# A decoder layer on one core: first stage in half chunks, gate sigmoids at the copies, HGRN products in 64x64 blocks, and moved transfers

## What is computed

```
ada = silu(c) @ w_ada + b_ada                      # sh1 sc1 gt1 sh2 sc2 gt2
h = x*(1+sc1) + sh1
qa ka va hq hf hi hg ga gb = split(h @ w_in)       # 7 x 512, 2 x 1024 columns
ya = attention(qa, ka, va)                         # 8 heads x 64, causal, ALiBi
yb = hgrn2(hq, hf, hi, hg)                         # 4 heads, chunks of 64 tokens, 128x128 state
mixed = sigmoid(ga)*(ya @ w_branch_a) + sigmoid(gb)*(yb @ w_branch_b)
x = layer_norm(ALPHA*x + gt1*(mixed @ w_out))
h2 = x*(1+sc2) + sh2
x = layer_norm(ALPHA*x + gt2*peer(h2))             # top 16 of 128^2 experts, 8 heads
```

## Time and profile before

| | |
|---|---|
| runs | 976.68, 977.14, 977.97 us; median 977.14 |
| profiled execution | 978.03 us; span in the profile 976.3 us |
| granted TensorE clock, mean | 0.994 |
| PE busy | 956.7 us, 98% |
| DVE busy | 802.2 us, 82% |
| ACT busy | 545.0 us, 56% |
| POOL busy | 385.4 us, 39% |
| DMA | 239.57 MB, mean 245 GB/s |
| chain that ended last | PE 88%, DVE 5%, DMA 3%, ACT 2% |

### The profile page before, as it was taken

How to read it: one execution, slowest core, us unless ns; L and a number is a source line. 1 busy time by engine, 2 the same in 40 slices (tenths; PEclk the granted TensorE clock), 3 DMA queues, 4 the chain that set the end, 5 groups by cost and what they waited for, 6 DMA issues and landing times.

```text
span 976.3 us, 17754 instructions
## 1 busy us (share of the span) xinstructions
PE 956.7 (98%) x6783; PEld 886.8 (91%) x6783; DVE 802.2 (82%) x1495; ACT 545.0 (56%) x851; POOL 385.4 (39%) x234
## 2 busy tenths in 40 slices
PE   8999999999999999999999999999999999999995
PEld 7999999999999999999999999888888888888884
DVE  6979888884987989887699998788776878887866
ACT  5477656455445464546577776554445444445542
POOL 1010101002888787676877867222330322300002
PEclk9999999999999999999999999999999999999998
DMA  9988968876666787886766666899889899986761
GB/s 358 412 300 270 352 200 326 311 222 219 195 201 179 196 200 176 217 198 185 179 159 167 157 169 152 290 323 316 284 288 369 300 327 333 324 293 215 216 193 44
DMA packets 86661, 239.57 MB, mean 245 GB/s; under 512 B 26929, under 2 KB 27953, under 8 KB 84913
## 3 DMA queue, kind: packets, MB, share of 16 engines
q1 hardware_dynamic: 59536, 207.94, 63.6%
q0 software_dynamic: 26752, 30.49, 13.5%
q10 hardware_dynamic: 288, 0.01, 0.0%
HBM read 227.84 MB, written 10.55 MB: 244 GB/s over the span
## 4 chain that ended last, share of the span: by engine, by line
PE 88%; DVE 5%; DMA 3%; ACT 2%; issue 1%; SPq 1%; POOL 1%; POOLq 0%; ACTq 0%; DVEq 0%
PE px L1303 35%; PE pw L964 15%; PE pw L965 15%; PE pw L966 15%; DMA raw<-in_ws 2%; DMA raw<-in_w 2%; DVE w_lo L1365 1%; PE px L1278 1%; PE px L1270 1%; PE px L965 1%; PE px L964 1%; PE px L966 1%; ACT oh_g L637 0%; PE px L1227 0%; ACT w_hi L637 0%
## 5 line engine op out<-in xcount | busy, mean ns | idle before, releaser
L637 ACT ACTIVATE w_hi<-raw 128x1024 fp32r<-128x1024 f32 x308 | 324.8, 1059 | 277.9 <-PE px L1303 144.8
L1365 DVE TENSOR_TENSOR w_lo<-raw,w_hi 128x1024 fp32r<-128x1024 f32 x285 | 348.1, 1229 | 87.5 <-ACT w_hi L637 84.9
L964 PE MATMUL pw<-a_hi,w_hi 128*128 128x240 f32 (+1 forms) x1248 | 347.2, 278 | 0.3 <-DVE a_lo L1617 0.3
L966 PE MATMUL pw<-a_hi,w_lo 128*128 128x240 f32 (+1 forms) x1248 | 344.5, 276 | 0.0
L965 PE MATMUL pw<-a_lo,w_hi 128*128 128x240 f32 (+1 forms) x1248 | 344.5, 276 | 0.0
L589 POOL DMA_INDIRECT gates_spill<-gate,place x128 | 237.2, 1853 | 72.6 <-issue 46.7
L964 PEld LDWEIGHTS pw<-a_hi,w_hi 128*128 128x128 f32 x1248 | 236.0, 189 | 1.8 <-issue 0.7
L965 PEld LDWEIGHTS pw<-a_lo,w_hi 128*128 128x128 f32 x1248 | 236.1, 189 | 0.0
L966 PEld LDWEIGHTS pw<-a_hi,w_lo 128*128 128x128 f32 x1248 | 236.0, 189 | 0.0
L1303 PE MATMUL px<-w_hi,ws_hi 128*128 128x512 f32 x512 | 159.0, 389 | 0.0
L1303 PE MATMUL px<-w_hi,ws_lo 128*128 128x512 f32 x512 | 158.9, 389 | 0.0
(11 more groups left out here) (370 smaller groups left out, 1277.8 us busy)
## 6 DMA issues: line engine op xcount, KB each, us to landing
raw<-in_u SPq DMA_DIRECT2D x128, 512.0 KB
raw<-in_v SPq DMA_DIRECT2D x128, 512.0 KB
raw<-in_ws SPq DMA_DIRECT2D x52, 512.0 KB
ada<-in_ada SPq DMA_DIRECT2D x20, 512.0 KB, 7.5
ada<-in_w_ada SPq DMA_DIRECT2D x16, 512.0 KB, 8.6
gates_spill<-zero POOLq DMA_DIRECT2D x16, 512.0 KB, 8.1
g_row<-gates_spill SPq DMA_DIRECT2D x32, 256.0 KB
raw<-in_w SPq DMA_DIRECT2D x7, 1024.0 KB, 11.8
```

Of the source, the lines that this page charges most:

```text
L637: return nc.scalar.activation(out, in_, ACT.Copy, **kw)
L964: nc.tensor.matmul(out, lh, rh, start=start and x == 0, stop=False)
L966: last = nc.tensor.matmul(out, ll, rh, start=False, stop=stop and x == len(pairs) - 1)
L1365: v.tensor_tensor(w_lo[:, m % RING], raw[:, m % RING], w_hi[:, m % RING].bitcast(F32), ALU.subtract).then_inc(lo_ready, 1)
```

## The change

- First stage: every chunk is copied and subtracted in two halves of 1024 columns. ACT's order per chunk is first half, a_hi and xT, second half; DVE's is modulation, first half, a_lo, second half. PE waits for the first half before the chunk and for the second before `first_rows`.
- Gates: gb is put through the sigmoid where it is copied out of PSUM; ga is still copied, and one sigmoid over all of it stands in ACT's iteration 20. The two sigmoids of iteration 23 go. DVE waits for each copy of gb.
- HGRN: the product at block 12 is made as 64x64 blocks on the diagonal (16 matmuls with 64 stationary and 64 moving columns for 8 of 128x128), and the state products at block 14 alternate between the two chunks.
- Transfers: x_nat and `ln_cols` load at block 20, after `s_done` 4 in place of `pv_done` 4; the bias of gt1 at block 21. AdaLN tiles: three in block 20, one in 21, 22 and 23 (before 1, 1, 2, 2). Of the 16 clears 0 to 6 stay; 7 to 15 are issued by POOL after each second subtraction of U, with no wait.
- `acc_lo` is made by DVE at block 21 instead of POOL. DVE's wait for the clears moves behind seven of its searches.

```diff
+X_AT = 20
...
-ADA_PER_BLOCK = {9: 2, 10: 1, 11: 1, 12: 1, 13: 1, 14: 2, 15: 2, 16: 2, 17: 2, 18: 2, 20: 1, 21: 1, 22: 2, 23: 2, 27: 1, 28: 1}
+ADA_PER_BLOCK = {9: 2, 10: 1, 11: 1, 12: 1, 13: 1, 14: 2, 15: 2, 16: 2, 17: 2, 18: 2, 20: 3, 21: 1, 22: 1, 23: 1, 27: 1, 28: 1}
...
-                    sp.wait_ge(lo1_ready, c - CHUNK_SLOTS + 2)
+                    sp.wait_ge(lo1_ready, 2 * (c - CHUNK_SLOTS) + 2)
...
-                if b == BRANCH + 2:
-                    sp.wait_ge(pv_done, HEADS // 2)
+                if b == X_AT:
+                    sp.wait_ge(s_done, HEADS // 2)
                     sp.dma_start(x_nat[:, :, :], x_d.rearrange("(a p) n -> p a n", p=P)).then_inc(x_landed, 16)
                     sp.dma_start(ln_cols[:, :], ln1_cols_d).then_inc(x_landed, 16)
+                if b == X_AT + 1:
...
-                    pool.wait_ge(lo_ready, 4 + 46 * n // ZERO_DMAS)
+                    if n < 7:
+                        pool.wait_ge(lo_ready, 4 + 46 * n // ZERO_DMAS)
...
-            clear(5, 10)
-            pool.wait_ge(o_done, TT)
-            pool.wait_ge(gt1_ready, 1)
-            nc.gpsimd.tensor_tensor(acc_lo[:, :], acc[:, :], acc_hi[:, :].bitcast(F32), ALU.subtract).then_inc(gt1_ready, 1)
-            clear(10, 12)
-
-            clear(12, 14)
+            clear(5, 7)
...
-            clear(14, ZERO_DMAS)
 
             pool.wait_ge(lo_ready, lo_count(UP - 1))
             for m in range(UP, UP + POOL_PIECES):
                 split_lo(m)
+                n = 7 + (m - UP) // 2
+                if (m - UP) % 2 and n < ZERO_DMAS:
+                    clear(n, n + 1)
...
-            def split_hi1(c):
-
-                act.wait_ge(raw1_landed[c % CHUNK_SLOTS], 16 * (c // CHUNK_SLOTS + 1))
+            def split_hi1(c, h):
+
+                q = slice(h * FW // 2, (h + 1) * FW // 2)
+                if c == 0 and h:
+                    act.wait_ge(raw1_head_landed, 16)
+                else:
+                    act.wait_ge(raw1_landed[c % CHUNK_SLOTS], 16 * (c // CHUNK_SLOTS + 1))
                 if c >= 2:
                     act.wait_ge(chunk_used, c - 1)
-                copy(hi1[c % 2][:, :], raw1[c % CHUNK_SLOTS][:, :]).then_inc(hi1_ready, 1)
+                copy(hi1[c % 2][:, q], raw1[c % CHUNK_SLOTS][:, q]).then_inc(hi1_ready, 1)
 
             for half in range(2):
                 act.wait_ge(sc_row_done, half + 1)
                 copy(sc_row[:, half * 512:(half + 1) * 512], (pw[0], px[0])[half][:, :]).then_inc(sc_row_ready, 1)
-            act.wait_ge(raw1_landed[0], 16)
-            copy(hi1[0][:, 0:FW // 2], raw1[0][:, 0:FW // 2]).then_inc(hi1_ready, 1)
             for c in range(KC):
+                split_hi1(c, 0)
                 act.wait_ge(x_chunk_landed[c], 16)
                 act.wait_ge(mod1_ready, c + 1)
                 for out in (a_hi, xT):
                     last = nc.scalar.activation(out[:, c], xT[:, c], ACT.Identity, scale=mod1[:, 2 * c + 1:2 * c + 2],
                                                 bias=mod1[:, 2 * c:2 * c + 1])
                 last.then_inc(h_hi_ready, 1)
-                if c == 0:
-                    act.wait_ge(raw1_head_landed, 16)
-                    copy(hi1[0][:, FW // 2:FW], raw1[0][:, FW // 2:FW]).then_inc(hi1_ready, 1)
-                if c + 1 < KC:
-                    split_hi1(c + 1)
+                split_hi1(c, 1)
...
-                for lo, dst in ((GA, sig_a), (GB, sig_b)):
-                    if lo <= e < lo + 4:
-                        r = e - lo
-                        copy(dst[:, 2 * r:2 * r + 2], pw[s][:, :].rearrange("p (c t) -> p c t", c=2)).then_inc(act_took, 1)
+                if GA <= e < GA + 4:
+                    r = e - GA
+                    copy(sig_a[:, 2 * r:2 * r + 2], pw[s][:, :].rearrange("p (c t) -> p c t", c=2)).then_inc(act_took, 1)
+                if GB <= e < GB + 4:
+                    r = e - GB
+                    nc.scalar.activation(sig_b[:, 2 * r:2 * r + 2], pw[s][:, :].rearrange("p (c t) -> p c t", c=2),
+                                         ACT.Sigmoid).then_inc(act_took, 1)
...
-                if b == 23:
-
-                    for dst in (sig_a, sig_b):
-                        act.wait_ge(act_took, evac_count(GB + 3))
-                        last = nc.scalar.activation(dst[:, :, :], dst[:, :, :], ACT.Sigmoid)
-                    last.then_inc(gates_ready, 1)
+                if b == 20:
+                    act.wait_ge(act_took, evac_count(GA + 3))
+                    nc.scalar.activation(sig_a[:, :, :], sig_a[:, :, :], ACT.Sigmoid).then_inc(gates_ready, 1)
...
-                pe.wait_ge(lo1_ready, c + 2 if c else 1)
+                pe.wait_ge(lo1_ready, 2 * c + 1)
                 pe.wait_ge(h_lo_ready, c + 1)
                 for b in range(HI):
                     first_block(b, c)
-                if c == 0:
-                    pe.wait_ge(lo1_ready, 2)
+                pe.wait_ge(lo1_ready, 2 * c + 2)
...
-                            q = slice(h * T + t * P, h * T + (t + 1) * P)
-                            last = nc.tensor.matmul(dst[:, h * P:(h + 1) * P], k_e[:, q], q_e[:, q], start=True, stop=True)
+                            for c in range(2):
+                                q = slice(h * T + t * P + c * CH, h * T + t * P + (c + 1) * CH)
+                                last = nc.tensor.matmul(dst[c * CH:(c + 1) * CH, h * P + c * CH:h * P + (c + 1) * CH],
+                                                        k_e[:, q], q_e[:, q], start=True, stop=True)
...
-                    for n in ((0, 1) if b == 14 else (2,)):
-                        dst = pv[n % 2]
-                        pe.wait_ge(kl_ready, 2)
-                        if n == 2:
-                            pe.wait_ge(state_ready, 1)
-                        t, q = n // 2, slice((n % 2) * CH, (n % 2 + 1) * CH)
-                        for h in range(HG):
-                            last = nc.tensor.matmul(dst[:, h * P:(h + 1) * P], kl_nat[q, t, h],
+                    chunks = (0, 1) if b == 14 else (2,)
+                    pe.wait_ge(kl_ready, 2)
+                    if b == 15:
+                        pe.wait_ge(state_ready, 1)
+                    for h in range(HG):
+                        for n in chunks:
+                            t, q = n // 2, slice((n % 2) * CH, (n % 2 + 1) * CH)
+                            last = nc.tensor.matmul(pv[n % 2][:, h * P:(h + 1) * P], kl_nat[q, t, h],
                                                     vh[q, t, h * P:(h + 1) * P], start=True, stop=True)
-                        last.then_inc(ds_done, 1)
+                            if h == HG - 1:
+                                last.then_inc(ds_done, 1)
...
-            modulation(0)
-            split_lo1_half(0)
             for c in range(KC):
+                modulation(c)
+                split_lo1(c, 0)
                 h_lo(c)
-                if c == 0:
-                    split_lo1_half(1)
-                if c + 1 < KC:
-                    modulation(c + 1)
-                    split_lo1(c + 1)
+                split_lo1(c, 1)
...
+                    dve.wait_ge(act_took, evac_count(GB + e - BRANCH))
...
+                if b == 21:
+                    dve.wait_ge(gt1_ready, 1)
+                    v.tensor_tensor(acc_lo[:, :], acc[:, :], acc_hi[:, :].bitcast(F32), ALU.subtract).then_inc(gt1_ready, 1)
...
-            dve.wait_ge(zero_landed, 16 * ZERO_DMAS)
...
+            dve.wait_ge(zero_landed, 16 * ZERO_DMAS)
```

More of the change, by code:

```diff
@@ L1380, in sum_ada, with split_lo1 @@
                 ins.then_inc(ada_done, 1)
-            def split_lo1(c):
-                dve.wait_ge(hi1_ready, c + 2)
+            def split_lo1(c, h):
+                q = slice(h * FW // 2, (h + 1) * FW // 2)
+                dve.wait_ge(hi1_ready, 2 * c + h + 1)
                 if c >= 2:
                     dve.wait_ge(chunk_used, c - 1)
-                v.tensor_tensor(lo1[c % 2][:, :], raw1[c % CHUNK_SLOTS][:, :], hi1[c % 2][:, :].bitcast(F32), ALU.subtract) \
+                v.tensor_tensor(lo1[c % 2][:, q], raw1[c % CHUNK_SLOTS][:, q], hi1[c % 2][:, q].bitcast(F32), ALU.subtract) \
                     .then_inc(lo1_ready, 1)
-            def split_lo1_half(h):
-                q = slice(h * FW // 2, (h + 1) * FW // 2)
-                dve.wait_ge(hi1_ready, h + 1)
-                v.tensor_tensor(lo1[0][:, q], raw1[0][:, q], hi1[0][:, q].bitcast(F32), ALU.subtract).then_inc(lo1_ready, 1)
             def modulation(c):
```

## The result

| | before | changed |
|---|---|---|
| median of the runs made together (6 each) | 977.05 us | 984.77 us |
| lowest and highest | 976.59, 979.25 | 983.64, 986.13 |
| profiled execution (span) | 978.03 (976.3) | 984.65 (982.9) |
| mean granted TensorE clock in it | 0.994 | 0.992 |

A forecast was written before the change was run, and what follows sets the result against it. TensorE, busy 98% of the span, was taken as the bound; gains of 1.25 + 0.95 + 3.3 less 0.1 make 5.4 us off 978.03, 972.6, so a median of 971.7; range 969.8 to 975.2.

The forecast's parts named there:

- Clears in U: Nine clear issues of 0.74 us in POOL's subtraction loop: 1.2 us behind, about 4 in hand, cost 0.
- a PE wait in U: Listed sign that the forecast is wrong: PE waiting in U, where no wait for w_lo was expected.
- The slower rival: In U, each clear issue costs POOL 2.24 us, not 0.74; PE waits 10.7 us, time 982.4; chance 0.04.
- First stage: Half copies and subtractions start chunks 1 and 2 earlier; first streamed block at 59.4 against 60.67, gain 1.25 us.
- The loop: First stage, DVE and ACT: 5.81 us a round against PE's 5.71, so chunks 3 to 7 start 0.1 apart.
- the new wait: End of first stage: ACT's weight copies start at 53.7, not 52.34; PE's first block waits for the bank until 59.4.
- HGRN: Blocks 12 and 14: 64x64 products take 1.35 us, gain 0.4; alternating state products gain 0.55; together 0.95.
- The middle: Blocks 19 to 24: m_lo wait of 1.8 us and low clock of 1.5 go, gain 3.3; y_lo loses 0.1.
- the sum: Whole kernel: 1.25 + 0.95 + 3.3 - 0.1 = 5.4 us gained, median 971.7.
- The DMA relief: From 150 to 176 us the DMA loses 4 MB of 9.5; its share falls from 0.98 to near 0.6.
- the m_lo step: Around block 24: DVE starts earlier, m_lo is ready at 189.0, 1.7 us early, so PE's 1.8 us wait goes.
- A2: Follow-up theory for U: POOL instructions overlapping 0.3 to 0.4 us shut DVE out; at 0.04 to 0.1 it gets in.

The follow-up runs named there:

- experiment 1: Changed kernel with the nine late clears issued by POOL in their old places ahead of U, all else as changed: 972.39 us, ratio 0.995.
- experiment 3: Changed kernel with the nine clears of U issued from SP's queue at the same points, POOL only subtracting: 972.32 us, ratio 0.9948.
- experiment 7: Changed kernel with one added wait: POOL's 15th subtraction of U waits for DVE's gates subtraction and place computation; clears stay in U: 972.34 us, ratio 0.995.
- experiment 8: Changed kernel, clears in U, with the gates' row maximum copied to PSUM and place_f kept there: 972.54 us, ratio 0.9946.
- experiment 9: Changed kernel with the nine clears issued by POOL in its idle stretch ahead of U: 972.14 us, ratio 0.9946 of the kernel before.
- experiment 12: Kernel before with only the sigmoids, moved transfers, three adaLN tiles and acc_lo on DVE, clears in old places: 974.85 us, ratio 0.9971.
- experiment 2: Kernel before with only the nine clears moved into U and DVE's wait for the clears moved: 987.71 us, ratio 1.0092.
- experiment 4: Changed kernel with clears before U and 704-column POOL memsets in their places in U: six runs 972.1 to 972.8, four 980.0 to 980.7, ratio 0.9979.
- experiment 5: Changed kernel with clears before U and nine 960-column POOL memsets in their places in U: median 985.53 us, ratio 1.0052.
- experiment 10: Kernel before with only the first stage in halves: 975.89 us, ratio 0.9985.
- experiment 11: Kernel before with only the 64x64 HGRN blocks and the alternating state products: 976.25 us, ratio 0.9996.
- experiment 6: Changed kernel with five of the nine clears issued before U and only the last four in it: 983.01 us, ratio 1.0053.

## Why the prediction was wrong

**The step that failed** is "Clears in U": "POOL falls 0.13 back a pair, 1.2 us in all, and has about 4 us in hand ... Cost 0, covered by that lead". Its numbers held: an issue's record is 0.7 to 1.1 us but takes 0.7 from start to start, a pair of POOL's takes 5.46 for the 5.51 of the forecast, and PE never waits for a piece of POOL. What failed is the cost put at 0: it asked who waits for POOL's results and not who needs POOL to stand still. The 0.6 us pauses of the earlier trace rows were taken for slack; in the kernel before they were where the gates subtraction and `place_f` got through (275.04 to 275.43, POOL paused from 274.82 to 275.40). Shut out of them, DVE came 21.4 us late out of `place`, its weight piece 11.3 late, PE stood 10.1 and lost 2.3 more by the clock. The cost was 12.4 us. The prediction's own list of what would show it wrong had "a PE wait in U", and that is what came, on the other engine's pieces.

**The slower rival** ("The clears starve POOL", 0.04, 982.4) had the clears and nearly the size, but the wrong way round: it had DVE hold up POOL's issues, which in U took 0.90 us in the median and 1.09 at most, not 2.24. That its 10.7 us of waiting are near the measured 10.1 is chance. Of the rule that it cited from the Trainium skill (SBUF — State Buffer, the "DVE blocks DMA" trap), no run here shows the effect; here GpSimd's stream held up VectorE.

**First stage.** PE's chunks 1 and 2 at 18.05 and 24.16 (18.24 and 24.47 forecast), first streamed block 59.24 (59.4). Chunk 0 began 0.36 earlier in this run (12.07, not 12.43); counted from it the block came at 47.17, for 46.97 forecast and 48.24 before: 1.07 gained for 1.25. The loop is as forecast: `a_hi` starts every 5.8 us from chunk 3 to 7. So is the new wait: ACT copies from 53.30 in place of 52.34, and PE starts 0.14 us after ACT has emptied the bank (59.10); the profile names the DVE subtraction that ended at 59.20, but that one is not of this block. Alone the part measures 1.24, with an interval of 0.5 to 2.3; that it is so near to 1.25 is luck.

**HGRN.** The products took 1.08, not 1.35: 0.034 a record, against 0.112 for the 128x128 form. The state products took the 1.09 read from the scores. By the rows 1.3 is gained, by the medians of the runs 0.88, which its ratio does not tell from no change; forecast 0.95. The products' cost was taken 0.3 too high. The factors are 1.7 and 1.5, under the 2 that the Trainium skill (TensorEngine Tiling (Array Packing), Theoretical Speedup) gives as the most.

**The middle.** The m_lo wait went and y_lo's stayed at 0.9 (1.0 forecast). By the medians the part is worth 2.3, 0.9 less than the forecast, which the interval (1.8 to 3.9) still holds. A likely reason is the low clock: 1.5 was taken from a single execution, and two other runs with nearly the same wait show none. The same may explain why the sum came out a little low: the profiled run was 0.9 above the median, and I took that off as well, though the low clock may be the very thing that made it longer. So a part of it would be counted twice. Where DVE is not shut out (experiments 1, 3, 7, 8 and 9) the kernel takes 972.1 to 972.5, against a forecast of 971.7; beside their own runs of the kernel before that is 5.0 to 5.6 less, for 5.4. All of the forecast but the clears thus came out, as far as these runs can tell.

**The DMA relief,** on which the m_lo step leaned ("Unknown is only whether weights arrive"), was not needed: with the clears in their old places (experiments 1 and 12) the share from 150 to 176 is still 0.90 (0.71 in the changed kernel, where near 0.6 was forecast), and there is no m_lo wait either. In experiment 2 the moved clears removed that wait by themselves. So either does, and beside the other edits the move of the late clears bought nothing.

**What stays open.** Why DVE sometimes gets in between two POOL instructions that follow each other (by the times, experiment 4 in six runs of ten, experiment 5 in one of ten) and in the changed kernel never did in six runs. The traces hold a hint that was not tested. POOL's records overlap, by 0.04 us where it has just paused and by up to 0.4 where clears stand between its subtractions. At ten boundaries the overlap was 0.04 us or less while one of the three operations waited (one each in the kernel before and in experiments 1, 3, 9, 10, 11 and 12, three in experiment 4), and DVE got in at all ten. At 0.06 us or more it was passed over 45 times (changed kernel 11, experiments 2, 4, 5, 6 and 7: 11, 1, 11, 10 and 1) and got in only beside a `memset` (0.10), at the issue of a clear (0.12), and in experiment 7, where POOL then stood still. So a weaker form of A2, in which the overlap matters from a much smaller size on, is not excluded. It would change which boundaries let DVE in, not that POOL's subtractions are what shuts it out.

## What to carry to other kernels

Before you fill an engine's pauses, ask not only who waits for its results but who uses the pauses. If two engines share a path, look in the trace of before for one operation with two durations at two places (here 2.42 and 0.23 us): the long one hints at the path, and its neighbour's pauses are then part of the schedule. Three cures were measured here, at 972.1 to 972.5 us each: put the filler where the engine is idle anyway, give one explicit wait, or keep one operand of the short operations in PSUM.

## What the runs showed of the hardware

- A DVE operation of 64 columns that needs the shared path stood 21.9 us while eight POOL subtractions and three issues began, all of them after its own start. That one operation can be passed over so often was not expected.
- Who is shut out: SBUF with two tensor inputs (21.89), and a TENSOR_SCALAR from SBUF to SBUF (21.39, 18.80). Not: the same two-input forms with one operand in PSUM (0.22), the TENSOR_SCALAR that writes to PSUM (0.28), and the maximum searches, whose means beside POOL's stream are the usual 0.28 and 0.43 us. The Trainium skill (GPSIMD Engine Reference, Specifications) names contention with two SBUF inputs or a 2-port mode; the trace agrees.
- Outcomes come in clusters. The kernel of experiment 4 has two times (972.1 to 972.8 and 980.0 to 980.7), that of experiment 5 several (972.0, 980.2, 985.0 to 986.8, 992.8), and a median over few runs can show any of them.
- The granted clock fell to 0.50 behind the wait of 10.1 us, and to 0.51 behind one of 1.75 us in the kernel before; behind waits of 1.55 and 1.74 us at the same place in two other runs it stayed at 1.00.
